# Two FFN-kernel rules changed together: where the first weight tiles of an FFN stand, and who carries product P1 into the bank of P2

## The reference

```python
def swiglu_ffn(x, w_gate_up, w_down):
    g, u = jnp.split(x @ w_gate_up, 2, axis=-1)
    return (jax.nn.silu(g) * u) @ w_down

for layer in range(DEPTH):
    x = x + FFN_RES * swiglu_ffn(rms_norm(x, ffn1_norm[layer]), ...)
    x = x + mixer(rms_norm(x, mix_norm[layer]))
    x = x + FFN_RES * swiglu_ffn(rms_norm(x, ffn2_norm[layer]), ...)
return rms_norm(x, final_norm)
```

## Time and profile before

| | us |
|---|---|
| median of 3 runs | 1818.45 (1818.11 to 1819.89) |
| the profiled execution | 1817.13 |
| its span in the profile | 1815.3 |
| mean granted TensorE clock | 0.985 of 2.4 GHz |
| TensorE busy | 1737.7 (96% of the span) |
| VectorE, ScalarE, GpSimd busy | 1413.1, 1010.9, 434.3 |

### The profile page before, as it was taken

One profiled execution on the slowest core, in us unless ns is written; L12 is line 12 of the kernel. 1 busy time (PEld: TensorE's weight loads), 2 busy tenths in 40 slices (PEclk: granted clock), 3 DMA queues, 4 the chain that ended last, 5 costly groups with the idle time before them and its releaser, 6 DMA issues. The chain is left out here.

```text
span 1815.3 us, 35301 instructions
## 1 busy us (share of the span) xinstructions
PE 1737.7 (96%) x12929; PEld 1625.4 (90%) x12929; DVE 1413.1 (78%) x2769; ACT 1010.9 (56%) x2008; POOL 434.3 (24%) x495
## 2 busy tenths in 40 slices
PE   7999999999989999999899999999999899999997
PEld 6899999977879999999899999987867799999986
DVE  4788787667758878877788788766897678878788
ACT  5564664446646646655665555544565556556452
POOL 1333333111013333330233333300000033333320
PEclk7999999999999999999999999999999999999999
DMA  6799989533429998995489989934112388998961
GB/s 176 160 202 208 215 193 207 149 113 91 128 63 201 205 207 193 204 227 150 103 192 199 218 197 208 210 90 125 29 40 59 113 174 195 208 211 196 205 148 61
DMA packets 170377, 293.80 MB, mean 162 GB/s; under 512 B 22689, under 2 KB 56670, under 8 KB 170206
## 3 DMA queue, kind: packets, MB, share of 16 engines
q0 software_dynamic: 66816, 121.66, 39.2%
q1 hardware_dynamic: 101824, 168.13, 30.0%
q10 hardware_dynamic: 1566, 1.74, 0.3%
HBM read 163.29 MB, written 2.10 MB: 91 GB/s over the span
## 5 line engine op out<-in xcount | busy, mean ns | idle before, releaser
L1957 PE MATMUL bank<-h_all,w_all 128*128 128x256 f32 x2352 | 675.5, 287 | 38.9 <-DVE w_all L1278 24.1
L1958 PE MATMUL bank<-h_all,w_all 128*128 128x256 f32 x2352 | 669.7, 285 | 0.0
L1959 PE MATMUL bank<-h_all,w_all 128*128 128x256 f32 x2352 | 669.5, 285 | 0.0
L790 POOL DMA_DIRECT2D work<-r_all x348 | 307.6, 1027 | 1000.2 <-DVE w_all L1278 615.5
L1957 PEld LDWEIGHTS bank<-h_all,w_all 128*128 128x128 f32 x2352 | 454.9, 193 | 49.6 <-DVE w_all L1278 36.0
L1958 PEld LDWEIGHTS bank<-h_all,w_all 128*128 128x128 f32 x2352 | 455.3, 194 | 0.0
L1959 PEld LDWEIGHTS bank<-h_all,w_all 128*128 128x128 f32 x2352 | 455.2, 194 | 0.0
L1278 DVE TENSOR_TENSOR w_all<-work,w_all 128x512 fp32r<-128x512 f32 x352 | 233.8, 687 | 110.2 <-ACT w_all L906 109.2
L1278 DVE TENSOR_TENSOR w_all<-r_all,w_all 128x512 fp32r<-128x512 f32 (+1 forms) x356 | 299.7, 863 | 14.1 <-ACT w_all L906 12.1
L906 ACT ACTIVATE w_all<-r_all 128x512 fp32r<-128x512 f32 (+1 forms) x356 | 267.7, 769 | 72.9 <-PE bank L1959 52.2
L906 ACT ACTIVATE w_all<-work 128x512 fp32r<-128x512 f32 x352 | 209.0, 622 | 112.8 <-DMA work<-r_all 63.2
(11 more groups left out here) (226 smaller groups left out, 2685.0 us busy)
## 6 DMA issues: line engine op xcount, KB each, us to landing
work<-r_all POOLq DMA_DIRECT2D x348, 256.0 KB, 4.6
r_all<-ffn_gu SPq DMA_DIRECT2D x88, 512.0 KB, 5.0
r_all<-r_all POOLq DMA_DIRECT2D x116, 256.0 KB, 6.5
r_all<-ffn_gu SPq DMA_DIRECT2D x88, 256.0 KB, 6.0
work<-ffn_gu SPq DMA_DIRECT2D x88, 256.0 KB, 5.3
r_all<-ffn_d SPq DMA_DIRECT2D x32, 512.0 KB, 4.9
x_f<-ffn_e SPq DMA_DIRECT2D x24, 384.0 KB, 5.1
work<-ffn_d SPq DMA_DIRECT2D x32, 256.0 KB, 4.1
```

Of the source, the lines that this page charges most:

```text
L790: pool.dma_start(chain[g % CHAIN], plain[(u + 2) % 3][:, part * S:(part + 1) * S], accum_op=ALU.add).then_inc(chain_sum[g % CHAIN], 16)
L1957: t.matmul(o, wh, xh, start=c == 0 and not on, stop=False, skip_group_check=on)
L1958: t.matmul(o, wh, xl, start=False, stop=False, skip_group_check=on)
L1959: last = t.matmul(o, wl, xh, start=False, stop=c == PAIRED - 1, skip_group_check=on)
```

## The change

1. **First tiles.** For f = 0, 1 and 3 (`shifted`), FA(0) goes to slot 3 (instead of 0), and FU(u) to slot 1+(u+1)%2 (instead of 1+u%2). FA(1) no longer waits for the plain unit; FE(1) and FD(1) wait for it instead. For f = 1 and 3 the first fills are FU and FC at step 5 and FA at step 6. The plain groups of f > 0 come in another order. `begin` has ScalarE's and VectorE's work of u = 1 in another order. P5(1) now stands ahead of P6(1).
2. **P1.** ScalarE copies P1 into bank 3, in all units, D units too. P2 waits for that copy (`e_1`) and adds to it (`start` is false; one extra matmul an FFN opens bank 3). VectorE's sum of P1 and P2 goes away, and `first_normed` multiplies bank 3 with `r_x` directly, behind the end of P2. D units lose VectorE's `x_added` of P1.
3. **Order.** P4(u-1) stands between P1(u) and P2(u).

```diff
 def product_order():
-    out = [(q, 0) for q in (2, 5, 4)] + [(q, 1) for q in (1, 2, 6, 5, 7)]
+    out = [(q, 0) for q in (2, 5, 4)] + [(q, 1) for q in (1, 2, 5, 6, 7)]
     for u in range(2, NU):
-        out += [(1, u), (2, u), (4, u - 1), (6, u), (3, u - 1), (5, u), (7, u)]
+        out += [(1, u), (4, u - 1), (2, u), (6, u), (3, u - 1), (5, u), (7, u)]
...
-PLAIN_ORDER = [(c, up) for c in range(PAIRED) for up in (False, True)]
+PLAIN_ORDER = [(0, False), (1, False), (2, False), (0, True), (3, False), (1, True), (2, True), (3, True)]
...
+        def first_order(f, j):
+            if f % 2:
+                return {5: (FU, FC), 6: (FA,)}.get(j, ())
+            return {4: (FA,), 5: (FU,), 6: (FC,)}.get(j, ())
...
-                if u >= ahead:
+                if u == 1 and kind in (FD, FE) and shifted(f):
+                    act.wait_ge(prod_done, product_count(f, 2, 0))
+                elif u >= ahead and not (u == 1 and kind == FA and shifted(f)):
...
-                    if gate:
-                        act.wait_ge(prod_done, product_count(f, 1, u))
+                    act.wait_ge(prod_done, product_count(f, 1, u))
+                    if at > 0:
                         act.wait_ge(e_2, at)
-                        a.activation(s_1, b[:, 0:HN], ACT.Copy).then_inc(e_1, 1)
+                    a.activation(D_BANK[:, 0:HN], b[:, 0:HN], ACT.Copy).then_inc(e_1, 1)
...
+            def first_normed(f, u, m):
+                at = order_of(f, u)
+                dve.wait_ge(misc_free, m + 2)
+                dve.wait_ge(prod_done, product_count(f, 2, u))
+                if u > 2:
+                    dve.wait_ge(e_4, at - 1)
+                elif f > 0:
+                    dve.wait_ge(e_4, order_of(f, 1))
+                v.tensor_tensor(g_0[u % 2], D_BANK[:, 0:HN], r_x[:, 0:HN], ALU.mult).then_inc(e_2, 1)
...
-                    elif q == 2 and at > 0:
-                        pe.wait_ge(e_2, at)
+                    elif q == 2:
+                        pe.wait_ge(e_1, at + 1)
...
-                    on = q in (3, 4, 6, 7)
+                    on = q in (2, 3, 4, 6, 7)
+                    if q == 1 and u == 1 and c == 0:
+                        t.matmul(D_BANK[:, 0:HN], wh, xh, start=True, stop=True)
```

More of the change, by code:

```diff
@@ L71, with first_fills, shifted, place_fa @@
 P_FILL = {1: FA, 2: FA, 6: FB, 5: FU, 4: FC, 3: FD, 7: FE}
+def first_fills(f):
+    plain = [FU, FC, FA] if f % 2 else [FA, FU, FC]
+    return [(k, 0) for k in plain] + [(k, 1) for k in ([FA, FU] if f == 0 else [FU, FA]) + [FB, FE]]
+FIRST_FILLS = [first_fills(f) for f in range(FFNS)]
+def shifted(f):
+    return int(f != 2)
+def place_fa(f, u):
+    return 3 if u == 0 and shifted(f) else 0
+def place_fu(f, u):
+    return 1 + (u + shifted(f)) % 2
 def fill_count(f, kind, u):
     if u < 2:
-        at = {FA: 0, FU: 1, FC: 2}[kind] if u == 0 else {FU: 3, FA: 4, FB: 5, FE: 6, FC: 9, FD: 10}[kind]
+        at = FIRST_FILLS[f].index((kind, u)) if (kind, u) in FIRST_FILLS[f] else {FC: 9, FD: 10}[kind]
     elif kind in (FU, FA):
@@ L644, in load_plain @@
                     sp.wait_ge(fill_lo, fill_count(fe, FC, ue))
+                    if ue == 0 and fe % 2:
+                        sp.wait_ge(fill_lo, fill_count(fe, FA, ue))
                     if ue > 0:
@@ L982, in pairs_out @@
                     high(n + j + AHEAD + 1, end)
-                    if 4 <= j < 7:
-                        high_fill(f, (FA, FU, FC)[j - 4], 0)
+                    for kind in first_order(f, j):
+                        high_fill(f, kind, 0)
                     if j == KD - 1:
@@ L1030, in silu @@
                 buf = g_1 if half else g_0[u % 2]
-                act.wait_ge(gr_done, half_count(f, u, half))
+                if half:
+                    act.wait_ge(gr_done, (TILES - 1) * f + UNITS[u][1])
+                else:
+                    act.wait_ge(e_2, order_of(f, u) + 1)
                 a.activation(buf, buf, ACT.Silu).then_inc(silu_done, 1)
@@ L1391, in pairs_out @@
                     low(n + j + AHEAD + 1, end)
-                    if 4 <= j < 7:
-                        low_fill(f, (FA, FU, FC)[j - 4], 0)
+                    for kind in first_order(f, j):
+                        low_fill(f, kind, 0)
                     if j >= 2 and j % 2 == 0:
@@ L1411, in first @@
                 def first():
[L1413 to L1414 removed]
                     low_fill(f, FA, 1)
                 def first_sums():
+                    low_fill(f, FA, 1)
                     mixed(0)
[L1420 removed]
+                    low_fill(f, FU, 1)
                     pair_mix(f, 2)
@@ L1428, in begin @@
                     rms_values(m, D, first_sums, sm[:, 0, 0, :])
-                    low_fill(f, FB, 1)
+                    pair_mix(f, 3)
                     mixed(2)
-                    pair_mix(f, 3)
                     mixed(3)
                 else:
+                    mixed(PAIRED - 1)
+                    low_fill(f, FU, 1)
                     rms_values(m, D, first)
-                    low_fill(f, FB, 1)
+                low_fill(f, FB, 1)
                 low_fill(f, FE, 1)
@@ L1575, in ffn @@
                     if gate:
-                        normed_gate(f, u, 0, m)
-                    if not gate:
+                        first_normed(f, u, m)
+                    else:
+                        c0 = UNITS[u][2]
                         dve.wait_ge(prod_done, product_count(f, 2, u))
-                        dve.wait_ge(e_1, at + 1)
                         x_added(c0, 0, D_BANK[:, 0:HN]).then_inc(e_2, 1)
@@ L2000, in ffn @@
                     spread(m + 1)
-                product(f, 6, 1, (0, 2))
+                product(f, 5, 1, (0, 2))
                 if f == 0:
                     spread(m + 1)
-                product(f, 6, 1, (2, PAIRED))
-                for q in (5, 7):
+                product(f, 5, 1, (2, PAIRED))
+                for q in (6, 7):
                     product(f, q, 1)
```

63 lines of the change are left out of this document (24 added, 39 removed).

## The result

The changed kernel takes 1850.46 us (median of 4 runs, 1847.05 to 1852.26) against 1819.12 before (4 runs): ratio 1.017, 95% interval 1.0152 to 1.0189. It is slower by 31 us. The forecast was slower, by 9, and its range ended at 1842. The profiled execution is the longest of the four.

What follows compares the result with a forecast made beforehand. TensorE, busy 96%, was taken as the bound, leaking at starts and behind mixed units. Starts -29.8, boundaries +38.7, extra matmuls +0.5, D units and ends nothing to -0.4: +9, so 1827.5 us, range 1806 to 1842.

Steps and rivals of the forecast that it cites:

- The starts: First plain group to P1(2) in each FFN: part 1 removes TensorE pauses, -29.8 us in all, bounds -15 and -35.
- What would be late next: At the starts: P2(1) at f = 0 waits for ScalarE to about 40.7; P7(1) at f = 1 about 1.7 late.
- Ordinary units and D units: Units not behind mixed ones: P4 and P2 don't wait; extra matmuls 0.5 us, D units and ends nothing to -0.4.
- The boundary at full clock: Unit behind a mixed one: P4 and P2 wait for copies, 2.47 us per boundary.
- the second step: Behind mixed units: P2's later end delays tile FA, VectorE, silu and the copy of P7 by 0.53 us.
- The 30.5 us of before: TensorE pauses of the kernel before, nearly all behind the 28 mixed units: 19.1 + 56 x 0.2 us.
- The step that failed: Behind mixed units: 2.47 us taken for all 28 boundaries, 69.2 against 30.5 before, so +38.7 us.
- the forecast's case: Whole kernel: the summed terms hold, 1820 to 1836 us, chance 0.46.
- rival C: New pauses before P4: clock falls in 11 of 28, +15, 1843 us, or backlog stays, +14; chance 0.13.
- the sign for being wrong that I had named: Behind P4's pauses at mixed-unit boundaries: a granted clock of 0.5 would show the prediction wrong.
- Rival A: Behind mixed units: shift goes and L1563's 0.42 us shortens the boundary to 1.6; kernel 1803 us, chance 0.19.
- waits for the copy of P1 (L1086): TensorE waits in the new profile: those for P1's copy appear with about 10 us.

Runs made afterwards that it cites:

- experiment 1: Changed kernel with 12 extra matmuls into an idle bank, read by nobody, before P4's wait behind the 28 mixed units: 1832.0 us, ratio 1.0075.
- experiment 5: Changed kernel with VectorE, in mixed units, taking tile FE ahead of the product behind P2 and the first sum ahead of tile FA: 1814.6 us, ratio 0.9979.
- kernel 3: Changed kernel with part 1 undone, but P5(1) still ahead of P6(1), so parts 2 and 3 alone: 1882.8 us, ratio 1.0352.
- kernel 4: Changed kernel with ScalarE copying P7 ahead of silu in mixed units: 1864.9 us, ratio 1.0243.
- kernel 6: Changed kernel with part 3 undone: P1 still copied into bank 3, but P2 directly behind P1: 1919.9 us, ratio 1.0559.

## Why the prediction was right and wrong

- **The starts** were forecast at -29.8 and came to -28.5: 31.9, 23.9, 25.1, 23.5 us where 31.4, 22.8, 25.7, 23.1 stood. What would be late next (P2(1) behind ScalarE at f = 0, P7(1) at f = 1) was late: P2(1) of f = 0 starts at 40.5 us (40.7 forecast), though P1(1) is there at 32.1, not 34.4, so it waits 6.9 us and not 4.8; P7(1) of f = 1 is 2.2 late (1.7 forecast).
- **Ordinary units and D units** cost next to nothing, as forecast: the 80 that are not behind a mixed unit take 2.2 us in all above 10.08 (0.1 before), 0.9 of them in u = 2 of f = 1, at half clock behind the start. The copy into bank 3 takes 0.37 us (116 copies, median 368 ns), like the copy of P1 into SBUF before (84 copies, median 372 ns). The Trainium skill, "ScalarE: Activation LUTs" (step by step: what each stage is for), has PSUM as the quicker target; at this shape no gain shows.
- **The boundary at full clock** was forecast at 2.47 us with its two steps (P4 too early for the copy of P7: 1.94; P2's later end, through tile FA and VectorE: 0.53). It measured 2.45 in front of G units (2.63 in front of D units, experiment 1), and experiment 5, which gives VectorE work during its wait for P2 and gets the copy of P7 0.6 earlier, shows that the second step has that cause. The 30.5 us of before are 31.2 by the pitch.
- **The step that failed** is "so I take 2.47 for all: 28 x 2.47 = 69.2". The clock was taken as full in the forecast's case, and its fall was left to rival C, with a chance of 0.13, in 11 of 28 boundaries, as something instead of the forecast. What the runs show in its place: the boundaries take 92.0 us, since the clock fell on top, in 18 of 28, at 1.2 to 1.3 us each, 22 to 23 us together, and experiment 1 takes them away without touching the pause's end. It is also the sign for being wrong that I had named: a granted clock of 0.5 behind P4's pauses. With these 22 to 23 us the forecast's +9 becomes +31 to +32, and 31 were measured. (This sum takes the clock's part as measured, so its fit checks only the other terms.)
- The rows that I had put 2 us between (full clock behind 1.6 us, half behind 2.4) could not decide it, and the trace of before had a closer pair that I did not put among them. P6(1) of f = 1 waits 2.3 us and runs at full clock behind it, while in the last unit of f = 3 a wait of 2.2 us for the copy of P7 is followed by half clock (windows of the kernel before, behind each pause):

```profile
543.90:546.50 2.60, 2.60 (x22) 2.60 (x23) 2.47 (x5) 2.57 (x3) 2.29 (x3) 1.00 0.94 162
1767.60:1770.20 2.60, 1.68 (x9) 1.39 (x7) 2.54 (x3) 0.00 (x0) 0.00 (x0) 0.50 1.00 375
```

So a pause of a little over 2 us was already seen to do either, and the two prices belonged into one sum for the 28 new pauses; with a fall at 1.4 us in every one the upper bound would have been 1827.5 + 39.2 = 1866.7.

- **Rival A** (VectorE's saved time shortens the boundary) is refuted in this kernel (it gave 1.6 us a boundary, 2.45 were measured): the time saved lies in front of the wait for P2. With VectorE's order changed as well (kernel 5) a boundary costs 1.85, below the 2.0 at which I had said that A decides; that is the order's doing, and how much of L1563's 0.42 us is in it is not shown.
- A small miss: waits for the copy of P1 (L1086) should have been about 10 us by name; the profile names 0.7, because a pause that costs 0.39 is drawn as 0.17 of idle time and put down to a tile.

## What to carry to other kernels

A product moved to the front of its unit must find its inputs there in the longest unit, not in the usual one: here 20 ordinary units of each FFN gained nothing and the 7 behind mixed ones paid. Before you forecast a new TensorE pause, price the pause and the half clock behind it as one term, and ask whether a small reordering on the engine that is waited for gets under it: the same pause of 2 us cost 2.45 in some places of the program and 3.5 to 3.9 in others. And look at what the engine could do in front of a new wait: two of VectorE's instructions in another place won 36 us, while for the one that the change takes out, which stood in front of that wait, no gain shows.

## What was not expected of the hardware

The clock's fall isn't decided by one pause alone: the same pause (P4 at +3.43, 1.8 us drawn idle) was followed by half clock in 18 of 28 boundaries of the changed kernel and in 16 of 28 in kernel 3, at other places of the program. Nor does the longer pause always do more: 1.9 us drawn idle in front of P2 (kernel 4) brought the clock down in 26 of 28, 2.2 us (kernel 6) in only 11 of 28, and 1.23 us (kernel 5) in none of 28. What tells the places apart is not shown. Nor does the half clock begin at once: in the 18 boundaries of the changed kernel it came 0.1 to 1.5 us behind P4's start, mostly after 8 to 12 matmuls at a pitch of 0.12 us, and the next 13 to 18 ran at 0.21. And matmuls that compute nothing of use made the kernel 18 us faster.
